# A two-block transformer kernel on one core: the conditioning's weights loaded partly ahead of x, and thirteen of its sums instead of eleven ahead of the first projection steps

## The reference

```python
c_act = jax.nn.silu(c)
mod = c_act @ w_ada[l] + b_ada[l]
shift, scale, gate = jnp.split(mod, 3, axis=-1)
h = _rms(x, norm_g[l]) * (1.0 + scale[:, None, :]) + shift[:, None, :]
proj = h @ w_in[l]
```

## Time and profile before

| what | us |
|---|---|
| median of 3 runs | 2596.74 (2596.69 to 2596.79) |
| the profiled execution's own time | 2597.67 |
| its span | 2596.4 |
| TensorE busy | 2580.0 |
| VectorE busy | 1028.8 |
| ScalarE busy | 1082.6 |
| GpSimd busy | 1140.5 |

### The profile page before, as it was taken

One profiled execution on the slowest core, in us unless ns is written; L12 is line 12 of the kernel. 1 busy time (PEld: TensorE's weight loads), 2 busy tenths in 40 slices (PEclk: granted clock), 3 DMA queues, 4 the chain that ended last, 5 costly groups with the idle time before them and its releaser, 6 DMA issues.

```text
span 2596.4 us, 33094 instructions
## 1 busy us (share of the span) xinstructions
PE 2580.0 (99%) x13414; PEld 2077.6 (80%) x13414; DVE 1028.8 (40%) x1622; ACT 1082.6 (42%) x1769; POOL 1140.5 (44%) x580
## 2 busy tenths in 40 slices
PE   8999999999999999999999999999999999999999
PEld 3778777877888888888888888888888888888887
DVE  3963444435444421344785343334333223312300
ACT  4334344444445432344444444444444444333311
POOL 0014444343434454543454444445555556554543
PEclk9999999999999999999999999999999999999999
DMA  9953333233333244422222333333333333333443
GB/s 398 389 176 111 106 99 113 82 118 102 122 102 114 86 134 146 126 89 81 90 81 86 106 99 100 103 100 106 102 107 119 120 110 111 119 108 115 148 145 104
DMA packets 97785, 322.84 MB, mean 124 GB/s; under 512 B 10977, under 2 KB 13025, under 8 KB 93025
## 3 DMA queue, kind: packets, MB, share of 16 engines
q1 hardware_dynamic: 92016, 301.16, 34.9%
q10 hardware_dynamic: 5616, 19.56, 2.0%
HBM read 303.90 MB, written 16.78 MB: 124 GB/s over the span
## 4 chain that ended last, share of the span: by engine, by line
PE 97%; DVE 3%; DMA 0%; ACT 0%; issue 0%; POOL 0%; SPq 0%; DVEq 0%; ACTq 0%
PE bank L824 28%; PE bank L826 28%; PE bank L825 28%; PE bank L767 2%; PE bank L1019 1%; PE bank L1008 1%; PE bank L939 1%; DVE TA L1610 1%; PE bank L1002 1%; PE bank L973 1%; DVE first L1610 1%; DVE wlo L1593 0%; PE bank L1055 0%; PE bank L1070 0%; PE bank L788 0%; PE bank L866 0%
## 5 line engine op out<-in xcount | busy, mean ns | idle before, releaser
L2127 POOL TENSOR_TENSOR wlo<-wraw,whi 128x1024 fp32r<-128x1024 f32 (+3 forms) x420 | 970.2, 2310 | 1318.4 <-ACT whi L1125 1318.2
L824 PE MATMUL bank<-Hhi,whi 128*128 128x512 f32 x2720 | 1093.6, 402 | 0.2 <-POOL Hlo L2231 0.2
L826 PE MATMUL bank<-Hhi,wlo 128*128 128x512 f32 x2720 | 1061.9, 390 | 0.0
L825 PE MATMUL bank<-Hlo,whi 128*128 128x512 f32 x2720 | 1060.5, 390 | 0.0
L1125 ACT ACTIVATE whi<-wraw 128x1024 fp32r<-128x1024 f32 (+3 forms) x438 | 440.5, 1006 | 685.9 <-PE bank L826 647.2
L824 PEld LDWEIGHTS bank<-Hhi,whi 128*128 128x128 f32 x2720 | 511.0, 188 | 113.8 <-issue 9.9
L826 PEld LDWEIGHTS bank<-Hhi,wlo 128*128 128x128 f32 x2720 | 510.6, 188 | 109.2
L825 PEld LDWEIGHTS bank<-Hlo,whi 128*128 128x128 f32 x2720 | 511.4, 188 | 103.5 <-issue 2.2
L824 PE MATMUL bank<-Ohi,whi 128*128 128x512 f32 x320 | 127.9, 400 | 0.0
L826 PE MATMUL bank<-Ohi,wlo 128*128 128x512 f32 x320 | 124.8, 390 | 0.0
L825 PE MATMUL bank<-Olo,whi 128*128 128x512 f32 x320 | 124.6, 389 | 0.0
(11 more groups left out here) (272 smaller groups left out, 2733.9 us busy)
## 6 DMA issues: line engine op xcount, KB each, us to landing
wraw<-in_w_in SPq DMA_DIRECT2D x293, 512.0 KB, 3.5
TA<-in_w_ada SPq DMA_DIRECT2D x22, 1024.0 KB, 17.1
first<-in_w_ada SPq DMA_DIRECT2D x32, 512.0 KB, 4.5
wraw<-in_w_out SPq DMA_DIRECT2D x32, 512.0 KB, 3.5
wraw<-in_w_o SPq DMA_DIRECT2D x32, 512.0 KB, 3.5
first<-in_w_ada SPq DMA_DIRECT2D x10, 1024.0 KB, 14.0
wmem<-in_w_mem ACTq DMA_DIRECT2D x16, 512.0 KB, 9.4
wraw<-in_w_beg ACTq DMA_DIRECT2D x16, 512.0 KB, 7.7
```

Of the source, the lines that this page charges most:

```text
L824: e.matmul(out, hi[:, c], xhi[k], start=first and j == 0, stop=False)
L825: e.matmul(out, hi[:, c], xlo[k], start=False, stop=False)
L826: m = e.matmul(out, lo[:, c], xhi[k], start=False, stop=last and end)
L2127: e.tensor_tensor(M.wlo[b][:, 0:w], M.wraw[b][:, 0:w], M.whi[b][:, 0:w].bitcast(F32), ALU.subtract).then_inc(S.lo)
```

## The change

The list of loads has pieces 0 to 2 ahead of x, pieces 3 and 4 between x1 and x2, and piece 5 and the rest in the old order behind x3. `START` ends with units 10, 11 and 12, with remainder 0 behind unit 10 and remainder 1 behind unit 12. `AHEAD` is 13, and `UNITS` gives nineteen units to the 16 steps instead of twenty-one: the steps with two are 8, 11, 14 and 15 instead of 6, 8, 10, 12, 14 and 15. Nothing is added to or taken from the work.

```diff
 START = [(x[0], int(x[1:])) for x in ("m0 m1 m2 m3 m4 m5 m6 m7 m8 m9 m10 m11 m12 m13 a0 a1 a2 a3 a4 a5 a6 a7 a8 a9 "
-                                      "m14 a10 m15").split()]
+                                      "a10 m14 a11 a12 m15").split()]
-AHEAD = 11
+AHEAD = 13
-UNITS = (0, 1, 1, 1, 1, 1, 2, 1, 2, 1, 2, 1, 2, 1, 2, 2)
+UNITS = (0, 1, 1, 1, 1, 1, 1, 1, 2, 1, 1, 2, 1, 1, 2, 2)
-LOADS = [(x[0], int(x[1:])) for x in ("x0 x1 x2 x3 " + " ".join(f"a{i}" for i in range(12)) + " k0 " +
+LOADS = [(x[0], int(x[1:])) for x in ("a0 a1 a2 x0 x1 a3 a4 x2 x3 " + " ".join(f"a{i}" for i in range(5, 12)) + " k0 " +
                                       " ".join(f"a{i}" for i in range(12, 32))).split()]
```

## The result

The changed kernel takes 2601.6 us (median of 19 runs, 2600.48 to 2603.03) where before takes 2597.01 (2596.55 to 2597.64): the ratio is 1.0018, interval 1.0011 to 1.0025, 4.6 us more. That lies within the 0.2% that the prediction counted as no change, near its upper edge as said, and the interval shows that it is slower all the same.

The account below looks back on a forecast made before the run. TensorE, busy 99% of the span, was taken as the bound, so the end follows its begun steps. 5.82 - 3.35 + 1.9 = +4.4 us on 2596.74 gave 2601.1 us, range 2599.0 to 2603.0.

Parts of the forecast that it names:

- Part 1: Loads ahead of the begun steps: the new order moves no piece from 5 on and costs nothing.
- The cover: ScalarE's squaring of x0: about 3 us of standing still lies inside its existing 4.16 us wait for TensorE.
- Part 2: VectorE ahead of TensorE's first begun step: two more sums and one remainder make it start 5.82 us later.
- Part 3: The sixteen begun steps: stalls fall from 5.55 to 2.2 us, winning back 3.35 us, give or take 0.4.
- the lead's account: Begun steps: VectorE's lead on TensorE gains 0.63 us per one-sum step, loses 1.71 per two-sum step, capped at 2.3.
- Part 4: TensorE's idle gap before the first begun step grows to 7.0 us; its slowed clock then costs 1.9 us.
- A clock that holds: Rival, gap before the first begun step: TensorE's clock doesn't fall; +2.5 us, 2599.2 us; chance 0.14.
- A clock that stays low for longer: Rival, first begun step: wholly at half rate it costs 5.44 us; +7.9 us, 2604.6 us; chance 0.16.
- Pieces that land sooner than the bytes allow: Rival, before the begun steps: added sums fit VectorE's idle time; -2.2 us, 2594.5 us; chance 0.04.
- steps without any stall: Rival, begun steps: a longer lead covers even the last two steps' stalls; +2.2 us, 2598.9 us; chance 0.04.

## Why the prediction was right

**Part 1, the load order at nothing: right.** The run with the load order alone has before's time and before's stalls. The cover was the one named: ScalarE waits for x0 and x2 in the changed kernel, and then still waits for TensorE. Its timeline answers the earlier trace rows:

```profile
29.71 0.63 ACT L1179 ACTIVATE first<-Y 128x512 f32<-128x512 f32 x1 [3.64 <-DMA Y<-in_xT]
...
37.09 0.63 ACT L1179 ACTIVATE first<-Y 128x512 f32<-128x512 f32 x1 [3.16 <-PE bank L731]
...
45.58 0.63 ACT L1179 ACTIVATE first<-Y 128x512 f32<-128x512 f32 x1 [5.70 <-DMA Y<-in_xT]
```

**Part 2, 5.82 us ahead of the first step: right, measured 5.74.** From sum 10's start to the first step it is 83.61 - 72.01 = 11.60 us against 78.56 - 72.70 = 5.86. The step itself came at 83.61 and not at 84.4 because this whole execution ran 0.7 us ahead at sum 10. That is not the load order's doing: with the old order sum 10 begins anywhere from 71.57 to 72.70 in the traces, with the new one from 72.01 to 72.62. With the same order of sums and sum 10 at 72.62, the run with the spread doubles started the first step at 84.23.

**Part 3, 3.35 us won back: right, measured 3.26.** Of 78.33 us from the second step to the last, 14 x 5.44 = 76.16 are work and 2.17 are lost; 2.2 was the forecast. The stall of the last step is the same 1.5 us as in the earlier trace rows. Spreading the doubles took 1.5 us off this stretch, where the lead's account said 1.3.

**Part 4, 1.9 us for the clock: the mechanism right, the size partly luck.** The fall of the clock was the cause named, and the runs with products in the gap show it. The price is 1.95 to 2.2 us in the medians, the forecast's size, and 2.81 in the profiled execution, above the 2.3 that I had put as the upper end; there the 0.9 us too much are nearly made up for by the start, which was 0.7 us early.

Drawing a line between a gap of 1.16 us and one of 8.11 had no ground. The row for 8.11 us was one draw of many: in the changed kernel's trace the idle time at the start is 7.72 us, and the first eight products take 12.91 - 7.72 = 5.19 us; with thirty products in the gap it is 7.44 us, and they take 13.96 - 7.44 = 6.52, more after a shorter idle time.

```profile
7.72 5.36 PE L767 MATMUL bank<-wmem,HF 128*128 128x512 f32 x8 [7.72 <-ACT HF L1156]
12.91 3.60 PE L741 MATMUL bank<-TA,one 128*128 128x512 f32 x8
```

```profile
7.44 6.68 PE L767 MATMUL bank<-wmem,HF 128*128 128x512 f32 x8 [7.44 <-DMA wmem<-in_w_mem]
13.96 3.60 PE L741 MATMUL bank<-TA,one 128*128 128x512 f32 x8
```

Over the eleven traces, before's among them, the price at the start ranges from 1.5 to 3.1 us after 7.4 to 8.1 us. Ahead of the begun steps, gaps of 5.56 and 6.71 us cost 7.41 - 5.56 = 1.85 and 1.95, those of 7.13 and 7.28 us 2.81 and 8.24 - 5.56 = 2.68. What fits all four is the time for which the clock was still at 0.50 after the work had begun, 3.9, 4.2, 6.0 and 5.7 us: each microsecond of it cost 0.47, as products spaced 0.43 us instead of 0.23 must. What sets that time in a given execution is open.

The prediction also took the clock row for one that doesn't show such a fall. But the earlier trace rows begins at 20 us and says nothing of the first products, and before's trace has no record of the clock until 12.6 us, where time without a record counts as 1.00. In the gap that the change opens the row does show 0.50.

**The rivals.** A clock that holds is what the 14 products make: 2599.65, where 2599.2 was worked out. A clock that stays low for longer did come, in part. The rival decided from a price of 2.7 us on, and the profiled execution has 2.81; low for the whole first step, 5.44 us, it was not. The granted clock is listed with every one of the changed kernel's 19 runs: six have a mean of 0.998, as the profiled one, and took 2602.22 to 2603.03 us, over 0.2% more than before; thirteen have 0.999 and took 2600.48 to 2601.98. So the median lies within the 0.2% because the shorter low stretch was the more frequent one, which the prediction could not know. Pieces that land sooner than the bytes allow, and steps without any stall, did not come.

The kernel before isn't free of this either: in the three rounds, seven of its 69 runs have a mean clock of 0.999 instead of 1.000 and take 2598.79 to 2599.47 us, some 2 us more, and so does the one run with 14 products that stands apart (2601.61). No trace of such a run was kept, so where the clock fell in them is not known.

## What to carry to other kernels

Work moved ahead of a start is free only if it fits idle time that is there for lack of order, not for lack of data: here the engines' bytes set when each piece came, so loading three of them early moved no later one. Ahead of the busiest engine's start each microsecond is paid in full, plus what the clock's fall costs, which varies from run to run, and the steps behind give back only the stalls that they had. Where an engine bounds a stretch by its total work, look for its own short waits: in the medians 2.2 us came from filling one of them and from placing the heavy steps so that the others didn't arise, though a change of that size is at the edge of what one measurement shows.

## What the runs showed of the hardware

GpSimd and VectorE blocked each other on plain fp32 work in on-chip memory: a remainder of 2.38 us took 4.15 behind a sum, a scaling of 0.75 took 2.87 behind that remainder. The Trainium skill, page "SBUF — State Buffer", section "SBUF: two separate sides", says that of a VectorE operation with two inputs in SBUF and a GpSimd operation that reads SBUF, whichever starts first holds the ports that they share for its whole instruction, and the other is blocked. The rows agree: the remainder ends 2.3 us after the sum does, and the scaling 0.5 us after the remainder. In the profile such a block shows as a long instruction and not as a wait.

TensorE's granted clock fell to 0.50 in the gaps of 5.6 to 7.3 us ahead of the first begun step, which then took 7.4 to 8.4 us instead of 5.56. In the run with GpSimd's remainders it fell at stalls of 4.4, 4.4 and 3.3 us, and a stall of 2.8 us left it at 1.00, as did the gaps and stalls of up to 1.5 us in the other traces. With 6.2 us of products of no use in the gap it held in ten of eleven runs (mean clock 1.000).
